# Storing the gated tile with a channel's four groups side by side, and reading its four shifted copies back in one transfer

## The chip, the cores and the metric

One core of one Trainium2 chip runs the whole kernel in one launch. The metric is device time in microseconds (us) of one execution, lower is better. Beside the plain timings there is one execution recorded by the hardware profiler; every row shown here is from that one. The engines are PE (matmul), DVE (vector), ACT (activation functions), POOL (a second elementwise engine) and SP, which here only issues transfers. A transfer issued by SP is spread over DMA engines, of which the core has 16.

## The reference, cut to what matters

Two layers of a diffusion transformer over 512 latent tokens and 256 context tokens, 1024 features, float32. The change touches the first layer's mixer alone, a convolution module that both streams pass through:

```
def conformer_conv(h, w_pw1, b_pw1, w_dw, b_dw, ln_g, ln_b, w_pw2, b_pw2):
    u = h @ w_pw1 + b_pw1
    a, g = jnp.split(u, 2, axis=-1)
    u = a * jax.nn.sigmoid(g)
    u = depthwise_conv(u, w_dw) + b_dw          # 31 taps per channel, over tokens
    u = jax.nn.silu(layer_norm(u, ln_g, ln_b))
    return u @ w_pw2 + b_pw2
```

After it come a gated feed-forward with a 3-tap convolution, then the second layer (neighbourhood attention and the same feed-forward).

## The kernel before

Everything is held with features on the 128 partitions and tokens along the row, so the 1024 features are 8 tiles. A matmul in float32 precision is made of three products of rounded parts (lines 1525 to 1527); for that ACT rounds every block of weights (`w_raw` to `w_hi`, line 757) and POOL makes the remainder (`w_lo`, line 611).

**The steps.** The first product and the convolution are run as 16 steps, `n` = 0 to 15: the 8 feature tiles of the context (256 tokens), then the 8 of the latents (512 tokens). In step `n` PE makes the two halves of the product (`pw1_step`, 2 x 24 matmuls), ACT takes the sigmoid of the second half, DVE multiplies it with the first into the gated tile `u` (`gated`, line 1247), and PE then does the convolution of the step before (`convolve(n - 1)`). In between PE does some unrelated matmuls for the modulation vectors, whose weights arrive as `ada_raw` (512 KB each, four buffers).

**The convolution.** A part of the 31 taps is done by PE, the rest by DVE directly on `u` (line 1223). On PE, four taps go in one matmul: the 128 rows of the moving operand are 32 channels in four copies, copy `i` shifted by `i` tokens, and the stationary operand `diag_w` holds the four taps on four 32-wide diagonals. A tile of 128 channels is four groups `j` of 32 channels, so a shifted buffer (`shifted_ctx`, `shifted_lat`, two of each) has partition `32 * i + b` and, in its row, the four groups `j` one behind the other. To bring channels `32 * j + b` onto partitions `32 * i + b`, SP stores `u` in DRAM (`u_dram`, two buffers a side) and reads it back four times.

**SP's order** is written by hand, `spread_u(n)`: wait for the gated tile (`glu`), wait that the last reading of this DRAM buffer has landed (`r_in`), store it, issue the two weight blocks of step `n + 3` (`step_loads`), wait until the store has landed (`u_out`), wait until the convolution two steps back has read its shifted buffer (`conv_pe`), issue the read-back, then issue up to two `ada_raw` loads. Ahead of the next `spread_u` there may be more `ada_raw` loads; together they are 3 a latent step and 1 a context step on average. All these transfers are on SP's one queue. `convolve(n)` waits for `r_in`.

Of the kernel before, what the change touches and what calls it, by code (L numbers as in the profile page):

```python
# [15 lines left out]
GROUPS, SHIFTS = 8, 4  # L16
PE_GROUPS = {"lat": 4, "ctx": 6}
DVE_TAP0 = SHIFTS * min(PE_GROUPS.values())
BLK32 = P // SHIFTS
# [5 lines left out]
LAT, CTX = "lat", "ctx"  # L25
# [46 lines left out]
def build(nc, shapes, rows_of, x_t, ctx_t, mod_w, mod_rows, cond_row, cv_w_pw1, cv_w_pw2, na_w_qkv, na_w_o, ffn_w_up, ffn_w_down,  # L72
          rpb_padded, vectors_in, taps_in, dve_taps_in, diag_in, ident_in, mask_in, out_t):
    L, C, D, F, HEADS, RPB_ROWS, RPB_COLS, TAPS = shapes
    N = {LAT: L, CTX: C}
    KD = D // P
    KF = F // P
# [83 lines left out]
    with stack:  # L161
        def sb(name, cols, dt=F32, on=stack):
            return on.enter_context(nc.sbuf_tensor(name, [P, cols], dt))

        def sem(name):
            return stack.enter_context(nc.semaphore(name))
# [45 lines left out]

        UW = {s: N[s] + 32 for s in N}
        RW = {s: N[s] + 28 for s in N}
        V, U, R, Yb, Ghi, Glo = {}, {}, {}, {}, {}, {}
        with ExitStack() as g:
            V[LAT], V[CTX] = sb("v_lat", KD * L, on=g), sb("v_ctx", KD * C, on=g)
            with ExitStack() as h:
                U[LAT] = [sb(f"u_lat{i}", UW[LAT], on=h) for i in range(2)]  # L220
                diag_w = [sb(f"diag_w{i}", GROUPS * SHIFTS * BLK32, on=h) for i in range(2)]
                taps_w = sb("taps_w", KD * GROUPS * SHIFTS, on=h)
                dve_taps = sb("dve_taps", KD * (GROUPS * SHIFTS - DVE_TAP0), on=h)
                diag = sb("diag", BLK32, on=h)
                glu_s = sb("glu_s", L, on=h)
                R[CTX] = [sb(f"shifted_ctx{i}", SHIFTS * RW[CTX], on=h) for i in range(2)]
                U[CTX] = [sb(f"u_ctx{i}", UW[CTX], on=h) for i in range(2)]
                R[LAT] = [sb(f"shifted_lat{i}", SHIFTS * RW[LAT], on=h) for i in range(2)]
                ada_raw = [sb(f"ada_raw{i}", 2 * 512, on=h) for i in range(ADA_RING)]
            with ExitStack() as h:  # L230
                Yb[LAT] = sb("yb_lat", KD * L, on=h)
                with ExitStack() as k:
                    Yb[CTX] = sb("yb_ctx", KD * C, on=k)
                Ghi[CTX] = sb("g_hi_ctx", KF * C, F32R, on=h)
                Glo[CTX] = sb("g_lo_ctx", KF * C, F32R, on=h)
            sb("first_room", KD * L + 2 * KF * C, on=g)
            ada_row = sb("ada_row", 512, on=g)
        with ExitStack() as g:
            Ghi[LAT] = sb("g_hi", KF * L, F32R, on=g)
# [1 line left out]
        with ExitStack() as g:  # L241
# [38 lines left out]
        u_dram = {s: [nc.dram_tensor(f"u_{s}_{i}", (P, UW[s]), F32, kind="Internal").ap() for i in range(2)]  # L280
                  for s in N}
# [4 lines left out]
        u_out = sem("u_out")  # L286
        r_in = {s: [sem(f"r_in_{s}{i}") for i in range(2)] for s in N}
# [130 lines left out]
        def side_of(n):  # L418

            return CTX if n < KD else LAT  # L420

        def pe_groups(n):

            return {STEPS - 1: GROUPS, STEPS - 2: GROUPS - 2}.get(n, PE_GROUPS[side_of(n)])
# [41 lines left out]
        def _(sp):  # L466
# [33 lines left out]
            def ada_loads(lists):  # L500
                for b in range(*lists):
                    if b + ADA_RING < CHUNKS * CHUNK_BLOCKS:
                        ada_load(b + ADA_RING)

            def spread_u(n):

                side, s, m = side_of(n), n % 2, n % KD
                uw, rw = UW[side], RW[side]
                sp.wait_ge(glu, n + 1)
                if m >= 2:  # L510
                    sp.wait_ge(r_in[side][s], 64 * (m // 2))
                sp.dma_start(u_dram[side][s][:, :], U[side][s][:, :]).then_inc(u_out, 16)
                step_loads(n + 3)
                sp.wait_ge(u_out, 16 * (n + 1))
                if n >= 2:
                    sp.wait_ge(conv_pe, n - 1)
                for i in range(SHIFTS):
                    d = u_dram[side][s]
                    src = bass.AP(tensor=d.tensor, offset=d.offset + i, ap=[[uw, BLK32], [BLK32 * uw, SHIFTS], [1, rw]])
                    dst = R[side][s][BLK32 * i:BLK32 * (i + 1), :].rearrange("p (j n) -> p j n", n=rw)  # L520
                    sp.dma_start(dst, src).then_inc(r_in[side][s], 16)
                ada_loads(ada_from[n][2])

            def step_loads(n):

                for half in range(2):
                    if n < STEPS:
                        ph = phases["pw1c" if n < KD else "pw1l"]
                        load(ph, n % KD // 2, 2 * (n % 2) + half, n % KD < 2)
                    else:  # L530
                        t = 2 * (n - STEPS) + half
                        load(phases["pw2c"], t // 4, t % 4, t < RING)
# [9 lines left out]
            for n in range(STEPS):  # L542
                for half in range(2):
                    ada_loads(ada_from[n][half])
                spread_u(n)
# [909 lines left out]
        def _(pe):  # L1455
# [27 lines left out]
            def convolve(n):  # L1483

                side, m, s = side_of(n), n % KD, n % 2
                w, rw = N[side], RW[side]
                pe.wait_ge(wd_rdy, n + 1)
                pe.wait_ge(r_in[side][s], 64 * (m // 2 + 1))
                if n >= 2:
                    pe.wait_ge(conv, n - 1)  # L1490
                groups = pe_groups(n)
                for g in range(groups):
                    for j in range(SHIFTS):
                        c = (g * SHIFTS + j) * BLK32
                        ins = pe.matmul(CONV[n % 2][BLK32 * j:BLK32 * (j + 1), 0:w], diag_w[s][:, c:c + BLK32],  # L1495
                                        R[side][s][:, j * rw + SHIFTS * g:j * rw + SHIFTS * g + w],
                                        start=(g == 0), stop=(g == groups - 1))
                ins.then_inc(conv_pe, 1)

            def pw1_step(n, extra=None):  # L1500

                ph, it, j = pw1_of(n)
                side = side_of(n)
                ready = normed("in_c" if side == CTX else "in_l") if n % KD == 0 else None
                for half in range(2):
                    split_wait(ph, it, j + half)
                    if half == 0 and n:
                        pe.wait_ge(glu, n)
                    products(bank[half][:, 0:N[side]], N[side], ph.slot(j + half), KD, Hhi[side], Hlo[side],
                             0, True, True, ready if half == 0 else None).then_inc(blk, 1)  # L1510
                    ada_products(ada_from[n][half])
                    if half == 0 and extra:
                        extra()
                if n:
                    convolve(n - 1)
                ada_products(ada_from[n][2])
# [180 lines left out]
            def last_convolution():  # L1697
                convolve(STEPS - 1)
                ada_turn(2)
# [158 lines left out]
            s = [ph.slot(j) for j in range(3)]  # L1858
# [107 lines left out]
```

## Time and profile before

| | us |
|---|---|
| median of 3 timed runs | 1746.15 |
| lowest and highest of them | 1746.05, 1753.84 |
| profiled execution | 1744.28 |
| its span, first to last instruction | 1742.5 |
| first store of a gated tile (step 0) | 62.83 |
| first store of a latent tile (step 8) | 159.32 |
| start of the last convolution (step 15) | 294.86 |
| PE busy, share of the span | 93% |

The 16 steps that the change touches thus lie in the first 305 us of the span. In the rows below a time is from the start of the span. The "DMA share" of a stretch is the busy share of the 16 DMA engines taken together (a packet's time can overlap the next one's, so it can come out slightly above 1), and GB/s is what they moved. PEclk is the granted TensorE clock as a part of 2.4 GHz.

### The profile page before, as it was taken

Reading aid. Unit: us, or ns where it says so; the run is one execution under the profiler, and the core shown is the slowest. Engines: PE = TensorE matmul, PEld = TensorE weight load, DVE = VectorE, ACT = ScalarE, POOL = GpSimd, SP = SyncE. Lnnn points to the kernel's source line nnn. Section 1 sums busy time; section 2 is a strip of 40 time slices with the busy share of each in tenths; the row PEclk is TensorE's granted clock in tenths of the full one; section 3 lists DMA queues with packets and bytes.
Section 4 is the critical chain, followed back from the end, with each engine's and each line's share of the span. In section 5 each row is a group of like instructions: output and inputs, shape, how many; then the busy total and the mean of one; then the engine's idle time right before and its main releaser. Section 6 shows DMA issues by size and latency. Waiting matters only on the chain.

```text
span 1742.5 us, 26261 instructions
## 1 busy us (share of the span) xinstructions
PE 1625.5 (93%) x9469; PEld 1310.2 (75%) x9469; DVE 712.8 (41%) x1396; ACT 748.8 (43%) x1126; POOL 791.0 (45%) x436
## 2 busy tenths in 40 slices
PE   4789998899899999999999799999987899999996
PEld 1666564779899988888888677788865788888884
DVE  0564796646662034444442524433342433333002
ACT  1532242546675445455322345444444444443220
POOL 0454334556679834444455334233326244444551
PEclk9899999999999999999999899999998899999998
DMA  7767787444456633233574111211203132333321
GB/s 250 274 202 218 213 236 218 157 146 130 145 172 180 184 97 96 97 90 91 226 278 161 50 37 50 79 42 43 67 25 109 49 97 96 96 96 89 96 81 49
DMA packets 70942, 222.63 MB, mean 128 GB/s; under 512 B 7888, under 2 KB 15568, under 8 KB 70608
## 3 DMA queue, kind: packets, MB, share of 16 engines
q1 hardware_dynamic: 69856, 219.91, 40.2%
q10 hardware_dynamic: 1008, 1.66, 0.3%
q8 instruction: 52, 0.85, 0.2%
q14 instruction: 26, 0.21, 0.0%
HBM read 216.03 MB, written 5.51 MB: 127 GB/s over the span
## 4 chain that ended last, share of the span: by engine, by line
PE 80%; issue 7%; DVE 5%; ACT 3%; DMA 2%; POOL 1%; DVEq 1%; ACTq 0%; SPq 0%; POOLq 0%
PE bank L1525 20%; PE bank L1527 20%; PE bank L1526 19%; PE bank L1735 3%; PE bank L1737 3%; PE bank L1736 3%; PE bank L1495 3%; PE bank L1813 2%; PE bank L1835 1%; PE bank L1823 1%; PE bank L1469 1%; DVE bank L1223 1%; PE bank L1665 1%; PE bank L1540 1%; DMA ada_raw<-in_mod_w 1%
## 5 line engine op out<-in xcount | busy, mean ns | idle before, releaser
L611 POOL TENSOR_TENSOR w_lo<-w_raw,w_hi 128x1024 fp32r<-128x1024 f32 (+1 forms) x284 | 668.3, 2359 | 810.0 <-ACT w_hi L757 809.8
L757 ACT ACTIVATE w_hi<-w_raw 128x1024 fp32r<-128x1024 f32 (+1 forms) x284 | 294.4, 1037 | 200.3 <-PE bank L1527 189.9
L1525 PE MATMUL bank<-h_hi_lat,w_hi 128*128 128x512 f32 x888 | 351.1, 395 | 5.1 <-DVE h_lo_lat L1182 4.5
L1527 PE MATMUL bank<-h_hi_lat,w_lo 128*128 128x512 f32 x888 | 349.4, 394 | 0.0
L1526 PE MATMUL bank<-h_lo_lat,w_hi 128*128 128x512 f32 x888 | 347.4, 391 | 0.0
L1525 PEld LDWEIGHTS bank<-h_hi_lat,w_hi 128*128 128x128 f32 x888 | 167.3, 188 | 53.6 <-issue 10.8
L1526 PEld LDWEIGHTS bank<-h_lo_lat,w_hi 128*128 128x128 f32 x888 | 167.2, 188 | 36.9
L1527 PEld LDWEIGHTS bank<-h_hi_lat,w_lo 128*128 128x128 f32 x888 | 167.2, 188 | 36.3
L1525 PE MATMUL bank<-h_hi_ctx,w_hi 128*128 128x256 f32 x560 | 166.8, 298 | 21.1 <-DVE g_lo_ctx L1367 10.2
L1526 PE MATMUL bank<-h_lo_ctx,w_hi 128*128 128x256 f32 x560 | 162.3, 290 | 0.0
L1527 PE MATMUL bank<-h_hi_ctx,w_lo 128*128 128x256 f32 x560 | 162.1, 289 | 0.0
L1527 PE MATMUL bank<-g_hi,w_lo 128*128 128x512 f32 x352 | 138.4, 393 | 0.0
L1525 PE MATMUL bank<-g_hi,w_hi 128*128 128x512 f32 x352 | 137.7, 391 | 0.0
L1526 PE MATMUL bank<-g_lo,w_hi 128*128 128x512 f32 x352 | 137.3, 390 | 0.0
L1525 PEld LDWEIGHTS bank<-h_hi_ctx,w_hi 128*128 128x128 f32 x560 | 111.4, 199 | 30.5 <-issue 13.0
L1354 DVE SCALAR_TENSOR_TENSOR bank<-gate_in,vectors,bank 128x512 f32<-128x512 f32 (+1 forms) x66 | 44.0, 666 | 170.4 <-ACT bank L911 170.0
L1526 PEld LDWEIGHTS bank<-h_lo_ctx,w_hi 128*128 128x128 f32 x560 | 111.0, 198 | 1.0 <-issue 1.0
L1527 PEld LDWEIGHTS bank<-h_hi_ctx,w_lo 128*128 128x128 f32 x560 | 111.1, 198 | 0.0
L1362 DVE TENSOR_TENSOR bank<-gate,bank 128x512 f32<-128x512 f32 (+1 forms) x66 | 40.1, 607 | 154.1 <-ACT gate L919 154.1
L1397 DVE CUSTOM_DVE_ANT_0 scores<-bank,bias 128x512 f32<-128x512 f32 x64 | 44.0, 687 | 103.3 <-issue 103.0
L1114 DVE RECIPROCAL root<-root 128x128 f32<-128x128 f32 x6 | 5.7, 953 | 190.3 <-ACT root L781 190.3
L637 POOL TENSOR_TENSOR feature_sum_lat<-feature_sum_lat,sq 128x512 f32<-128x512 f32 x32 | 41.8, 1306 | 88.2 <-ACT sq L883 88.1
(192 smaller groups left out, 2690.8 us busy)
## 6 DMA issues: line engine op xcount, KB each, us to landing
w_raw<-in_ffn_w_up SPq DMA_DIRECT2D x132, 512.0 KB, 3.6
ada_raw<-in_mod_w SPq DMA_DIRECT2D x64, 512.0 KB, 5.6
w_raw<-in_cv_w_pw SPq DMA_DIRECT2D x48, 512.0 KB, 5.1
w_raw<-in_ffn_w_down SPq DMA_DIRECT2D x48, 448.0 KB, 3.5
mod_rows<-in_mod_rows SPq DMA_DIRECT2D x32, 512.0 KB, 5.6
w_raw<-in_ffn_w_down SPq DMA_DIRECT2D x24, 512.0 KB, 3.7
w_raw<-in_na_w_qkv SPq DMA_DIRECT2D x24, 512.0 KB, 5.7
shifted_lat<-u_lat SPq DMA_DIRECT2D x32, 270.0 KB, 6.8
```

The lines of the kernel that those rows point to most:

```text
L611: pool.tensor_tensor(wlo[s][:, 0:kt * P], raw[s][:, 0:kt * P], whi[s][:, 0:kt * P].bitcast(F32), ALU.subtract).then_inc(w_lo, 1)
L637: pool.tensor_tensor(acc[side][:, :], acc[side][:, :], src, ALU.add).then_inc(done, 1)
L757: act.activation(whi[s][:, 0:kt * P], raw[s][:, 0:kt * P], ACT.Copy).then_inc(w_hi, 1)
L1354: dve.scalar_tensor_tensor(tp, g_in[:, 0:n], vcol("ffn_w_dw", m + layer * 3 * KF), tp, ALU.mult, ALU.add).then_inc(tap, 1)
L1397: dve.tensor_tensor_reduce(out=scores[par][:, :], in0=SCORES[hp][:, :], in1=bias[hp][:, n * 512:(n + 1) * 512], scale=1.0, scalar=-3e38, o ...
L1495: ins = pe.matmul(CONV[n % 2][BLK32 * j:BLK32 * (j + 1), 0:w], diag_w[s][:, c:c + BLK32], R[side][s][:, j * rw + SHIFTS * g:j * rw + SHIFT ...
L1525: pe.matmul(b, whi[s][:, w], hi[:, a], start=(first and k == 0), stop=False)
L1526: pe.matmul(b, whi[s][:, w], lo[:, a], start=False, stop=False)
L1527: ins = pe.matmul(b, wlo[s][:, w], hi[:, a], start=False, stop=(last and k == kts - 1))
L1735: pe.matmul(b, whi[s][:, w], hi[:, a], start=(k == 0), stop=False)
L1736: pe.matmul(b, whi[s][:, w], lo[:, a], start=False, stop=False)
L1737: ins = pe.matmul(b, wlo[s][:, w], hi[:, a], start=False, stop=(k == KD - 1))
```

## The change

The DRAM copy is laid out channel by channel, a channel `b`'s four groups `j` side by side (each `uw` long: 288 numbers for the context, 544 for the latents), where it was laid out like the tile. The store has the same 128 rows in SBUF; on the DRAM side it is now a pattern of 4 by 32 rows. The read-back is one transfer in place of four: 128 rows of `4 * uw - 4` numbers (4592 bytes for the context, 8688 for the latents) in place of 4 x 128 rows of `uw - 4` numbers (1136 and 2160 bytes). Its DRAM side is a pattern of 4 shifts by 32 channels, its SBUF side the 128 partitions. The semaphore `r_in` then rises by 16 a tile and not by 64, the step from group to group in a shifted buffer is `uw` and not `uw - 4`, and the shifted buffers are 12 numbers wider.

```diff
-        RW = {s: N[s] + 28 for s in N}
+        RW = {s: SHIFTS * UW[s] - SHIFTS for s in N}
...
-                uw, rw = UW[side], RW[side]
+                uw, d = UW[side], u_dram[side][s]
                 sp.wait_ge(glu, n + 1)
                 if m >= 2:
-                    sp.wait_ge(r_in[side][s], 64 * (m // 2))
-                sp.dma_start(u_dram[side][s][:, :], U[side][s][:, :]).then_inc(u_out, 16)
+                    sp.wait_ge(r_in[side][s], 16 * (m // 2))
+                rows = bass.AP(tensor=d.tensor, offset=d.offset, ap=[[uw, SHIFTS], [SHIFTS * uw, BLK32], [1, uw]])
+                sp.dma_start(rows, U[side][s][:, :]).then_inc(u_out, 16)
                 step_loads(n + 3)
                 sp.wait_ge(u_out, 16 * (n + 1))
                 if n >= 2:
                     sp.wait_ge(conv_pe, n - 1)
-                for i in range(SHIFTS):
-                    d = u_dram[side][s]
-                    src = bass.AP(tensor=d.tensor, offset=d.offset + i, ap=[[uw, BLK32], [BLK32 * uw, SHIFTS], [1, rw]])
-                    dst = R[side][s][BLK32 * i:BLK32 * (i + 1), :].rearrange("p (j n) -> p j n", n=rw)
-                    sp.dma_start(dst, src).then_inc(r_in[side][s], 16)
+                src = bass.AP(tensor=d.tensor, offset=d.offset,
+                              ap=[[1, SHIFTS], [SHIFTS * uw, BLK32], [1, SHIFTS * uw - SHIFTS]])
+                sp.dma_start(R[side][s][:, :], src).then_inc(r_in[side][s], 16)
...
-                w, rw = N[side], RW[side]
+                w, rw = N[side], UW[side]
...
-                pe.wait_ge(r_in[side][s], 64 * (m // 2 + 1))
+                pe.wait_ge(r_in[side][s], 16 * (m // 2 + 1))
```

SP's queue, steps 3 and 4 (context). A row gives the line, the tile written and read, and the shape on the written side. Before:

```order
L512 DMA u_ctx<-u_ctx 128x288 [waits r_in_ctx1,glu]
L479 DMA w_raw<-in_cv_w_pw 128x1024 [waits w_lo] x2
L521 DMA shifted_ctx<-u_ctx 32x4x284 [waits conv_pe,u_out]
L521 DMA shifted_ctx<-u_ctx 32x4x284 x3
L498 DMA ada_raw<-in_mod_w 128x1024 [waits ada_blk] x2
L512 DMA u_ctx<-u_ctx 128x288 [waits r_in_ctx0,glu]
```

With the change:

```order
L513 DMA u_ctx<-u_ctx 4x32x288 [waits r_in_ctx1,glu]
L479 DMA w_raw<-in_cv_w_pw 128x1024 [waits w_lo] x2
L520 DMA shifted_ctx<-u_ctx 128x1x1148 [waits conv_pe,u_out]
L498 DMA ada_raw<-in_mod_w 128x1024 [waits ada_blk] x2
L513 DMA u_ctx<-u_ctx 4x32x288 [waits r_in_ctx0,glu]
```

Three issues a step are gone, and nothing else has changed its place. The store writes 4 x 32 rows where it wrote 128; the read-back writes all 128 partitions at once.

SP's queue, steps 9 and 10 (latents). Before:

```order
L512 DMA u_lat<-u_lat 128x544 [waits glu]
L479 DMA w_raw<-in_cv_w_pw 128x1024 [waits w_lo] x2
L521 DMA shifted_lat<-u_lat 32x4x540 [waits conv_pe,u_out]
L521 DMA shifted_lat<-u_lat 32x4x540 x3
L498 DMA ada_raw<-in_mod_w 128x1024 [waits ada_blk] x2
L512 DMA u_lat<-u_lat 128x544 [waits r_in_lat0,glu]
```

With the change:

```order
L513 DMA u_lat<-u_lat 4x32x544 [waits glu]
L479 DMA w_raw<-in_cv_w_pw 128x1024 [waits w_lo] x2
L520 DMA shifted_lat<-u_lat 128x1x2172 [waits conv_pe,u_out]
L498 DMA ada_raw<-in_mod_w 128x1024 [waits ada_blk] x2
L513 DMA u_lat<-u_lat 4x32x544 [waits r_in_lat0,glu]
```

The same holds here. The `bias_table` loads of the attention, which the change doesn't touch, are the only transfers of the program before with a pattern like that of the new read-back: 8 by 16 rows in DRAM, 128 partitions of one row of 265 numbers in SBUF.

```
src = bass.AP(tensor=rpb_padded.tensor, offset=it * (4 * RPB_HEAD) + (2 * j + hp) * RPB_HEAD,
              ap=[[RPB_COLS, P // NA_KW], [1, NA_KW], [1, RUN]])
sp.dma_start(table[:, hp * RUN:(hp + 1) * RUN], src).then_inc(tab_in, 16)
```

## Rows read from the trace of the kernel before

**Rows 1.** The page: the span, busy time by engine, and 40 slices.

```profile
span 1742.5 us, 26261 instructions
...
PE 1625.5 (93%) x9469; PEld 1310.2 (75%) x9469; DVE 712.8 (41%) x1396; ACT 748.8 (43%) x1126; POOL 791.0 (45%) x436
...
PE   4789998899899999999999799999987899999996
...
DMA  7767787444456633233574111211203132333321
```

**Rows 2.** Longest waits of PE from 60 to 305 us: total us, times, longest.

```profile
PE bank L1495 <- issue: 15.5, 4, 4.5
PE bank L1525 <- POOL w_lo L611: 2.9, 1, 2.9
```

**Rows 3.** Chain of waits in that stretch, the waits at convolutions: start, us, what.

```profile
92.27 3.03 issue
...
113.17 3.73 issue
...
136.66 4.22 issue
...
290.32 4.54 issue
```

**Rows 4.** Timeline of SP's queue: start, us, line, tiles, count. First and last steps.

```profile
62.83 0.33 SPq L512 DMA_DIRECT2D u_ctx<-u_ctx  x1
...
85.45 0.33 SPq L512 DMA_DIRECT2D u_ctx<-u_ctx  x1
...
90.17 1.75 SPq L521 DMA_DIRECT2D shifted_ctx<-u_ctx  x4
...
159.32 0.33 SPq L512 DMA_DIRECT2D u_lat<-u_lat  x1
...
230.44 0.33 SPq L512 DMA_DIRECT2D u_lat<-u_lat  x1
```

**Rows 5.** Timeline of PE: two convolutions of latent steps.

```profile
212.46 3.64 PE L1495 MATMUL bank<-shifted_lat,diag_w 128*32 128x512 f32 x32
...
228.84 3.64 PE L1495 MATMUL bank<-shifted_lat,diag_w 128*32 128x512 f32 x32
```

**Rows 6.** Transfers by kind: count, KB each, median us from issue to landing.

```profile
w_raw<-in_cv_w_pw SPq DMA_DIRECT2D x48, 512.0 KB, 5.1
...
shifted_lat<-u_lat SPq DMA_DIRECT2D x32, 270.0 KB, 6.8
shifted_ctx<-u_ctx SPq DMA_DIRECT2D x32, 142.0 KB, 4.5
...
u_lat<-u_lat SPq DMA_DIRECT2D x8, 272.0 KB, 2.3
...
bias_table<-in_rpb_padded SPq DMA_DIRECT2D x16, 132.5 KB
```

**Rows 7.** Stretches: bounds, length, busy by engine, PEclk, DMA share, GB/s.

```profile
166.00:168.00 2.00, 2.00 (x13) 0.72 (x11) 0.01 (x1) 0.80 (x1) 0.00 (x0) 1.00 1.07 213
...
1203.00:1205.00 2.00, 2.00 (x13) 1.41 (x10) 1.78 (x8) 0.61 (x2) 0.00 (x0) 1.00 0.96 389
...
1161.00:1162.30 1.30, 1.30 (x8) 1.04 (x7) 1.18 (x6) 1.09 (x3) 0.74 (x1) 1.00 0.47 94
1234.90:1235.90 1.00, 1.00 (x6) 0.82 (x5) 0.90 (x5) 0.81 (x3) 0.70 (x1) 1.00 0.45 92
```

**Rows 8.** Timeline of SP's queue around the third of these stretches.

```profile
1159.58 1.46 SPq L491 DMA_DIRECT2D bias_table<-in_rpb_padded  x2
1161.60 1.50 SPq L479 DMA_DIRECT2D w_raw<-in_na_w_qkv  x3
```

**Rows 9.** Two stretches of the context steps, columns as in rows 7.

```profile
130.00:141.00 11.00, 6.78 (x68) 6.11 (x64) 6.83 (x11) 5.13 (x8) 5.73 (x4) 1.00 0.86 261
141.00:152.00 11.00, 11.00 (x80) 6.98 (x77) 7.09 (x10) 0.81 (x2) 3.64 (x2) 0.84 0.52 146
```

More of the change, by code:

```diff
@@ L225, in build @@
                 glu_s = sb("glu_s", L, on=h)
-                R[CTX] = [sb(f"shifted_ctx{i}", SHIFTS * RW[CTX], on=h) for i in range(2)]
+                R[CTX] = [sb(f"shifted_ctx{i}", RW[CTX], on=h) for i in range(2)]
                 U[CTX] = [sb(f"u_ctx{i}", UW[CTX], on=h) for i in range(2)]
-                R[LAT] = [sb(f"shifted_lat{i}", SHIFTS * RW[LAT], on=h) for i in range(2)]
+                R[LAT] = [sb(f"shifted_lat{i}", RW[LAT], on=h) for i in range(2)]
                 ada_raw = [sb(f"ada_raw{i}", 2 * 512, on=h) for i in range(ADA_RING)]
@@ L235, in build @@
                 Glo[CTX] = sb("g_lo_ctx", KF * C, F32R, on=h)
-            sb("first_room", KD * L + 2 * KF * C, on=g)
+            sb("first_room", KD * L + 2 * KF * C + 32, on=g)
             ada_row = sb("ada_row", 512, on=g)
```

## The prediction

> **What bounds the kernel now.** I read the page first: PE is busy for 93% of a span of 1742.5 us, and the slices show where it is not: among the few below 9 tenths are the first seven, and there the DMA engines are at 7 tenths and more [rows 1]. The change lies in exactly this part. Then the list of PE's waits between 60 and 305 us: 15.5 us in 4 waits stand at line 1495, the convolution, more than at all other lines together [rows 2]. The chain of waits gives their places, three in context steps and one before the last convolution, and calls them "issue", that is, no single releaser [rows 3]. Two rows of SP's queue say what the second half of it is: in step 2 the store goes out at 85.45 and the read-back only at 90.17, since SP waits for the store to land, and the convolution begins at 92.27 + 3.03 = 95.30, when the last of four readings has landed [rows 3, 4]. So the store and the read-back are already the late ones in four of 16 steps.
>
> One lap, from the first store (62.83) to the last convolution (290.32 + 4.54 = 294.86), takes 232.0 us: 96.5 us for the 8 context steps, 12.1 each, and 135.5 us for the 8 latent steps, 16.9 each [rows 3, 4]. This is the stretch that the change can lengthen or shorten.
>
> **What the change saves.** Three issues a step on SP: four take 1.75 us, so about 1.3 us of SP's time, of which 0.4 may be lost again, because the two issues of the similar bias_table pattern take 1.46 us, 0.73 each [rows 4, 8]. The read-back also leaves the form in which it fills only 32 partitions at a time. While those run, 213 GB/s are moved at a share of 1.07, 213 / (1.07 x 16) = 12.4 GB/s for each busy engine; weight blocks that fill all 128 partitions go at 389 / (0.96 x 16) = 25.3 GB/s [rows 7]. The copies' bytes are the same but for 12 numbers a row. PE, DVE, ACT and POOL have the same instructions of the same shapes, so I cost the wider step between groups and the moved buffers at nothing: a convolution reads the same 512 numbers a row and keeps its 3.64 us [rows 5].
>
> **What the change costs.** Both new transfers have a DRAM side whose outermost count is 4: the store 4 x 32 rows, the read-back 4 x 32. No transfer of before has that. The nearest is bias_table: outermost count 8 on the DRAM side, 128 partitions in SBUF. Two stretches show it in flight alone. It is issued at 1159.58, the weights behind it at 1161.60, and from 1161.0 to 1162.3 the DMA engines are busy 0.47 of the time (had the weights begun to arrive, the share would only be too high); at 1234.9 it is 0.45 [rows 7, 8]. Weights, with 128 as outermost count on both sides, show 0.96. I read this as: 8 of the 16 engines work on it, one for each outermost step, and the new transfers will be worked on by 4.
>
> The Trainium skill says so outright ("DMA: Bandwidth & Descriptors", section "Why a DMA increments its semaphore by 16 and not by 1"): a DMA runs on the largest number of engines, up to 16, that divides the slowest dimension of both sides, and on this path on the lowest-numbered ones. By that rule both transfers use the same 4 engines; the trace's 0.47 and 0.45 agree with its 8 for bias_table. The same page's list "Rules for kernel authors" also advises one large transfer for many small ones; by that alone the sum would be the second rival's below.
>
> Now the load on one of these 4 engines in one step, by bytes. Every 512 KB block (2 of weights, and ada_raw 3 times a latent and once a context step) [rows 6] is spread over all 16, 32.8 KB each, 1.30 us at 25.3 GB/s: 6.5 us a latent step, 3.9 us a context step. The store is 32 rows of 2176 bytes on each of the 4, 69.6 KB (context 32 x 1152 = 36.9 KB). The read-back is 32 rows of 8688 bytes, 278 KB (context 32 x 4592 = 147 KB). Before, they were 17 and 69 KB.
>
> The pace of a busy engine is the disputed price. At best it is the 25.3 GB/s of the weights: a latent step is then 6.5 + 2.8 + 11.0 = 20.3 us, a context step 3.9 + 1.5 + 5.8 = 11.2 us. At worst it is the 12.4 of the readings that crowd into 32 partitions, or the 94 / (0.47 x 16) = 12.5 and 92 / (0.45 x 16) = 12.8 of bias_table [rows 7]: latent 6.5 + 5.6 + 22.2 = 34.3, context 3.9 + 3.0 + 11.8 = 18.7. Each of the 4 engines would walk down a block of 32 partitions, side by side. bias_table is the nearest row in form, but its rows have 1060 bytes, and the trace has no long rows in that form, so I take 15 GB/s, near the slow end: latent 6.5 + 4.6 + 18.5 = 29.6, context 3.9 + 2.5 + 9.8 = 16.2.
>
> Is this load on the path? All is on one queue, so each engine works it off in order. SP issues the store of step n + 1 when PE has done the products after convolution n - 1: 228.84 - 212.46 = 16.4 us from convolution to convolution, and 230.44 - 228.84 = 1.6 us more to the store, 18.0 us [rows 4, 5]. Convolution n - 1 starts when read-back n - 1 has landed. From that landing the 4 engines have a whole step's work before them, 29.6 us, and the next store comes after 18.0: they never run empty, and a latent step takes what their load takes. The latency between store and read-back (a store now lands 2.3 us after its issue, of which most is not transfer [rows 6]) is covered by the two weight blocks behind the store, 2.6 us. In a context step it is 12.1 against 16.2, the same. The next weights still come in time, since they lie ahead of the read-back and are wanted two steps later.
>
> The sum: 8 x 16.2 + 8 x 29.6 = 366 us in place of 232, with nothing to give it back later, because PE is the bound from 305 us on and its work is the same. That is +134 us. The profiled execution, 1744.28 us (span 1742.5), would become 1878; the median of the runs is 1.9 above it, 1746.15 + 134 = **1880 us**.
>
> PE will idle in these steps. Its granted clock may then be below 1 for a part: in before, a stretch with 6.78 of 11 us busy is followed by one at 0.84 [rows 9]. At 0.84 the 18.0 us become about 21, still below 29.6, so I add nothing. If the pace is the fast one, this cover is gone, and it could cost up to 1 us a latent step.
>
> **The rivals.**
> 1. *Four engines, at the full pace.* The blocks do not get in each other's way, since engines drift apart. For it speaks that the rows are long. Context steps then stay at their 12.1, latent ones take 20.3: 96.5 + 162 = 259, +27, **1773 us**; with the clock's price 1781.
> 2. *All 16 engines share it, faster than before.* The mechanism would be that the SBUF side's 128 partitions decide, and bias_table's 0.47 comes from its short rows. Then the read-back goes at 16 x 25.3 = 405 GB/s over all partitions, 1.45 us instead of 2.8 in a context step and 2.75 instead of 5.2 in a latent step, and 1.2 us earlier by the issues saved. It takes 2.5 us from three waits and 3.7 from the fourth, which are 3.03 to 4.54 long [rows 3]: -11 us, **1735 us**. The point from which it decides is the engine count: with 8 engines at full pace the latent read-back takes 5.5 us, as long as now; only above that is there a gain. Against it: those two shares, since short rows would make a busy engine slow, not idle.
> 3. *The middle.* With 8 engines the latent load is 6.5 + 11.6 = 18.1 us, about PE's lap, and the context load 10: a little over PE's 16.9, near **1750 us**.
>
> **How the numbers follow.** Four engines near the slow pace 0.60, at the full pace 0.26, all 16 engines 0.10, something near no change 0.04. The likeliest gives 1880. Its bounds are 12.5 GB/s (8 x (18.7 + 34.3) = 424, +192, 1938) and the first rival (1773); both cases hold 0.86, so the range is 1773 to 1940. A change below 0.5%, 9 us, is about what a measurement of this kernel can't tell from none. Faster by more than that is rival 2, 0.10; within it rival 3, 0.04; slower 0.86.
>
> **What would show it.** In the profile after: DMA share in the read-back's stretches at 0.25 to 0.35 and some 60 GB/s, where now it is above 1 at 213; latent stores about 30 us apart; landing of shifted_lat 15 us and more; PE's waits at the convolution in nearly all 16 steps, 130 us in sum; from the second product on, nothing changed. A share near 1 and a landing under 5 us would prove the step on the engine count wrong; stores 20 us apart the step on the pace.

## The result: 8.2% slower

| | median us | ratio to before, 95% interval |
|---|---|---|
| before, the same chips | 1746.85 | |
| with the change | 1889.96 (1884.2 to 1898.4, 6 runs) | 1.0821 [1.0791, 1.0852] |

The forecast was 1880 us in a range of 1773 to 1940. The profiled execution of the change has a span of 1889.7 us, 147.2 more than before.

The page of the changed kernel: the span, the busy time by engine, and 40 slices of the span in tenths of busy time. They answer to [rows 1].

```profile
span 1889.7 us, 26213 instructions
...
PE 1650.1 (87%) x9469; PEld 1315.5 (70%) x9469; DVE 715.3 (38%) x1396; ACT 748.6 (40%) x1126; POOL 789.3 (42%) x436
...
PE   4757656567998999999999979999999699999996
...
PEclk9888877788999999999999989999999799999998
DMA  7554565554434465332328721121121222333321
```

The instruction counts of the engines are those of before. What has changed is the first quarter: PE is at 5 to 7 tenths in slices 2 to 9 (about 47 to 425 us), and the DMA engines, far from being fuller, are down to about 5 tenths. Both sides idle. This fits a transfer that a few engines carry while the others have nothing to do; the stretches below show it.

Longest waits of PE from 60 to 460 us (in total, times, longest), which answer to [rows 2]:

```profile
PE bank L1494 <- issue: 135.2, 12, 16.6
PE bank L1494 <- DMA shifted_ctx<-u_ctx: 4.7, 1, 4.7
PE bank L1524 <- POOL w_lo L610: 4.2, 1, 4.2
```

15.5 us in 4 waits have become 139.9 us in 13, all at the convolution (line 1495 is 1494 now). The difference, 124 of the 147 us, is the change's cost seen from PE. Most of the rest goes with PE's clock: PE was busy 24.6 us more (1650.1 against 1625.5) with the same 9469 matmuls, and the granted clock is lower in the slices in which it waits.

The chain of waits in the same stretch (start, us, what), two of the waits and the convolutions behind them; compare [rows 3]:

```profile
274.02 9.74 issue
283.75 5.27 PE bank L1494 x32
...
421.99 15.74 issue
437.73 8.51 PE bank L1494 x64
```

And SP's queue (start, us, line, tiles), which answers to [rows 4]:

```profile
61.18 0.68 SPq L513 DMA_DIRECT2D u_ctx<-u_ctx  x1
...
189.38 0.55 SPq L513 DMA_DIRECT2D u_lat<-u_lat  x1
...
256.21 0.54 SPq L520 DMA_DIRECT2D shifted_lat<-u_lat  x1
...
337.19 0.55 SPq L513 DMA_DIRECT2D u_lat<-u_lat  x1
...
366.96 0.55 SPq L513 DMA_DIRECT2D u_lat<-u_lat  x1
...
415.77 0.54 SPq L520 DMA_DIRECT2D shifted_lat<-u_lat  x1
```

The lap from the first store to the last convolution is 437.73 - 61.18 = 376.5 us, where it was 232.0: +144.5, nearly all of the 147.2. The context steps take (189.38 - 61.18) / 8 = 16.0 us each (12.1 before), the latent ones (437.73 - 189.38) / 8 = 31.0 (16.9 before). The first two latent stores are 16.0 us apart, and from the second on each comes 27.8 to 35.7 us after the one before; the pair shown is 29.8. The last read-back, issued at 415.77, lets PE go at 437.73, 22.0 us later. The one issued at 256.21, with more queued ahead of it, takes until 283.75.

Stretches of the changed kernel in which little else is in flight (bounds, length, busy by engine, PEclk, DMA share, GB/s), to be held against [rows 7]:

```profile
174.00:176.00 2.00, 2.00 (x27) 1.15 (x20) 0.50 (x1) 0.00 (x0) 0.00 (x0) 0.89 0.25 79
...
274.00:276.00 2.00, 0.02 (x1) 0.00 (x0) 0.75 (x1) 1.95 (x3) 0.24 (x1) 1.00 0.25 61
424.00:426.00 2.00, 0.00 (x0) 0.00 (x0) 0.00 (x0) 1.99 (x6) 0.74 (x2) 1.00 0.23 74
```

A share of 0.25 is 4 engines of 16. At 61 GB/s each of the four moves 15 GB/s, at 74 it is 74 / (0.23 x 16) = 20, at 79 in a context step 20.

Three more stretches show what the read-back's own do not:

```profile
223.00:227.00 4.00, 4.00 (x26) 1.25 (x19) 0.29 (x1) 0.00 (x0) 0.00 (x0) 0.67 0.26 102
415.40:417.00 1.60, 1.60 (x16) 0.93 (x9) 0.76 (x2) 0.00 (x0) 0.00 (x0) 1.00 0.11 46
186.60:190.50 3.90, 3.90 (x58) 2.38 (x60) 0.75 (x1) 2.00 (x3) 0.90 (x1) 1.00 0.00 0
```

In the first, a read-back has landed (PE went on at 220.45) and the next is issued only at 227.99; the four engines carry the store and what is left of the loads, at 102 / (0.26 x 16) = 25 GB/s each. In the second, a store has landed and the read-back that waited for it is just being issued: fewer than two engines are busy on average. In the third, at the end of the context steps, nothing is in flight at all.

### The profile page after: what moved, and what is told of

It is laid out like the page before. It is cut to its first block, busy times and chain, and to the rows that moved or that the text cites. A ratio compares the mean times of both kernels' runs of the same rounds, so it can differ in the third digit from the quotient of the medians.

```text
span 1889.7 us, 26213 instructions
## 1 busy us (share of the span) xinstructions
PE 1650.1 (87%) x9469; PEld 1315.5 (70%) x9469; DVE 715.3 (38%) x1396; ACT 748.6 (40%) x1126; POOL 789.3 (42%) x436
## 4 chain that ended last, share of the span: by engine, by line
PE 77%; issue 12%; DVE 3%; ACT 3%; DMA 3%; POOL 1%; DVEq 1%; ACTq 0%; POOLq 0%
PE bank L1524 19%; PE bank L1526 18%; PE bank L1525 18%; PE bank L1494 4%; PE bank L1734 3%; PE bank L1736 3%; PE bank L1735 3%; PE bank L1812 2%; PE bank L1468 2%; PE bank L1834 1%; PE bank L1822 1%; PE bank L1664 1%; PE bank L1539 1%; DMA ada_raw<-in_mod_w 1%; ACT w_hi L756 1%
## 5 line engine op out<-in xcount | busy, mean ns | idle before, releaser
L1524 PE MATMUL bank<-h_hi_lat,w_hi 128*128 128x512 f32 x888 | 351.7, 396 | 4.5 <-DVE h_lo_lat L1181 4.5
L1494 PE MATMUL bank<-shifted_lat,diag_w 128*32 128x512 f32 x304 | 52.6, 858 | 102.5 <-issue 102.5
L1524 PEld LDWEIGHTS bank<-h_hi_ctx,w_hi 128*128 128x128 f32 x560 | 110.8, 198 | 32.2 <-issue 15.5
L1494 PEld LDWEIGHTS bank<-shifted_lat,diag_w 128*32 128x32 f32 x304 | 13.5, 150 | 137.4 <-issue 137.4
```

Source lines behind the costliest of these rows:

```text
L1524: pe.matmul(b, whi[s][:, w], hi[:, a], start=(first and k == 0), stop=False)
```

## The experiments

All but e5 and e6 compute what the reference does; those two read back rows that the convolution does not want, and are there for their times alone. Ratios are to the kernel before, run beside them (its median was 1749.59 us beside e1 to e4 and 1748.66 beside e5 to e8). A lap is the time from the first store to the start of the last convolution in the profiled execution. The rest of the span is 1507 to 1518 us in all ten profiles, so the laps hold the large differences, but one of some us in a single profile says little: e4's lap is 3.6 us shorter than before's, its span 4.1 us longer, and its profiled execution was the slowest of its seven.

| kernel | store, engines | read-back, engines | median us | ratio | lap us |
|---|---|---|---|---|---|
| before | 1 issue, 16 | 4 issues, 16 | 1746.85 | | 232.0 |
| the change | 1, 4 | 1, 4 | 1889.96 | 1.0821 | 376.5 |
| e1_store_only | 1, 4 | 4, 16 | 1763.43 | 1.0088 [1.0062, 1.0114] | 246.4 |
| e2_read_only | 4, 16 | 1, 4 | 1864.07 | 1.0658 [1.0606, 1.0711] | 351.7 |
| e3_both16 | 4, 16 | 4, 16 | 1751.27 | 1.0009 [0.9983, 1.0035] | 239.1 |
| e4_order32 | 4, 16 | 1, 16 | 1740.11 | 0.9938 [0.9917, 0.9960] | 228.4 |
| e5_two_engines | 4, 16 | 1, 2 | 1925.37 | 1.0997 [1.0965, 1.1029] | 409.4 |
| e6_eight_engines | 4, 16 | 1, 8 | 1782.39 | 1.0189 [1.0158, 1.0221] | 264.9 |
| e7_order32_store4 | 1, 4 | 1, 16 | 1748.91 | 0.9992 [0.9975, 1.0010] | 236.5 |
| e8_short128 | 1, 16 | 4, 16 | 1741.18 | 0.9954 [0.9935, 0.9974] | 226.8 |

The engine counts are the theory's (the largest number up to 16 that divides the outermost counts of both sides); the stretches show 2, 4, 8 and 16.

The trace also records each packet, the piece that one engine moves at a time, and here a row of a store or of a read-back is one packet. Its time gives the pace of one busy engine without any dividing by a share. These are medians over the 16 steps:

| kernel | latent read-back row | GB/s | context read-back row | GB/s |
|---|---|---|---|---|
| before: 32 partitions at a time, 16 engines | 2160 bytes, 174 ns | 12.4 | 1136 bytes, 81 ns | 14.0 |
| e3: the same, long rows | 8688 bytes, 649 ns | 13.4 | 4592 bytes, 325 ns | 14.1 |
| the change: 128 partitions, 4 engines | 8688 bytes, 652 ns | 13.3 | 4592 bytes, 184 ns | 25.0 |
| e6: 128 partitions, 8 engines | 8688 bytes, 698 ns | 12.4 | 4592 bytes, 255 ns | 18.0 |
| e5: 128 partitions, 2 engines | 8688 bytes, 331 ns | 26.2 | 4592 bytes, 178 ns | 25.8 |
| e4: 128 partitions, 16 engines | 8688 bytes, 328 ns | 26.5 | 4592 bytes, 178 ns | 25.8 |
| e8: 128 partitions, 16 engines | 2160 bytes, 88 ns | 24.5 | 1136 bytes, 51 ns | 22.3 |

The latent store's row of 2176 bytes takes 91 ns in before, 89 ns on the change's 4 engines, and 143 to 153 ns where it goes in four issues of 32 partitions (e2, e3, e4).

**e1_store_only**, against the change: the read-back in four issues, still of long rows (the waits for `r_in` count to 64 again; here and below such changes of counts are left out of the cuts shown).

```diff
-                src = bass.AP(tensor=d.tensor, offset=d.offset,
-                              ap=[[1, SHIFTS], [SHIFTS * uw, BLK32], [1, SHIFTS * uw - SHIFTS]])
-                sp.dma_start(R[side][s][:, :], src).then_inc(r_in[side][s], 16)
+                for i in range(SHIFTS):
+                    src = bass.AP(tensor=d.tensor, offset=d.offset + i, ap=[[SHIFTS * uw, BLK32], [1, SHIFTS * uw - SHIFTS]])
+                    sp.dma_start(R[side][s][BLK32 * i:BLK32 * (i + 1), :], src).then_inc(r_in[side][s], 16)
```

> The store as in the change (4 by 32 rows on the DRAM side), the read-back in four transfers again, each of 32 long rows whose outermost count is 32. If the number of engines is the outermost count, only the store runs on 4 engines: 69.6 KB on each, 3 us where it took 1, so the 4 engines carry about 15 us a latent step against PE's 16.9 and are not the bound; the store only lands 1 to 3 us later, which counts in the steps where the convolution waited already. Expected 1750 to 1770 us. If the store were the costly half, it would be most of the 144 us: above 1850.

Measured 1763.43 us, inside. The store alone, with the layout, costs 0.88%; against e3, which has the layout too, it is 0.8%. How it costs is seen on SP's queue:

```profile
161.98 0.52 SPq L513 DMA_DIRECT2D u_lat<-u_lat  x1
162.54 1.12 SPq L479 DMA_DIRECT2D w_raw<-in_cv_w_pw  x2
169.58 1.72 SPq L520 DMA_DIRECT2D shifted_lat<-u_lat  x4
```

The read-back goes out 7.6 us after the store, where in step 12 of before it was 2.4 us (230.44 to 232.82). The list of SP's waits has it for all eight latent steps, 47.9 us of waiting for the store to land; in before the same row is 7.3 us:

```profile
SPq L520 <- DMA u_lat<-u_lat: 47.9, 8, 6.3
```

```profile
SPq L521 <- DMA u_lat<-u_lat: 7.3, 8, 1.0
```

I had expected the store to land 1 to 3 us later; it is (47.9 - 7.3) / 8 = 5.1. What was missing is that the two weight blocks issued right behind it use the same four engines before it is through. Its rows run from 163.14 to 169.21 us by the packet records, with packets of the weight blocks between them, and towards the end little more than four engines are busy, at the full pace:

```profile
167.00:169.00 2.00, 2.00 (x10) 1.63 (x10) 1.56 (x4) 0.00 (x0) 0.00 (x0) 1.00 0.29 99
```

The store's 69.6 KB and the weights' 2 x 32.8 KB on one engine are 5.3 us at 25.3 GB/s (an estimate), where the store alone would be 2.8.

**e2_read_only**, against the change: the store in four issues of 32 partitions.

```diff
-                rows = bass.AP(tensor=d.tensor, offset=d.offset, ap=[[uw, SHIFTS], [SHIFTS * uw, BLK32], [1, uw]])
-                sp.dma_start(rows, U[side][s][:, :]).then_inc(u_out, 16)
+                for j in range(SHIFTS):
+                    rows = bass.AP(tensor=d.tensor, offset=d.offset + j * uw, ap=[[SHIFTS * uw, BLK32], [1, uw]])
+                    sp.dma_start(rows, U[side][s][BLK32 * j:BLK32 * (j + 1), :]).then_inc(u_out, 16)
...
-                sp.wait_ge(u_out, 16 * (n + 1))
+                sp.wait_ge(u_out, 64 * (n + 1))
```

> The read-back as in the change (one transfer, 4 by 32 rows on the DRAM side), the store in four transfers of 32 partitions, which gives each an outermost count of 32. By the theory the 4 engines lose the store's 2.2 us a latent step and 1.2 a context step of the 31.0 and 16.0 measured: about 345 us from first store to last convolution, 1855 to 1870 us. By the rival, that the order of the rows in DRAM or their length is what costs and not the engine count, it would be the same as the change, 1890, or fall only with e3.

Measured 1864.07 us, inside. The read-back is the costly half, 6.6%; with e1's 0.9% they make 7.5 of the 8.2%.

**e3_both16** has both edits: the change's layout and its long rows, all with outermost count 32.

> The change's layout in DRAM and its long rows, but store and read-back each in four transfers of 32 partitions, outermost count 32. If engine count is all, this is the time of before within 0.5%: 1740 to 1756 us, perhaps a few us more for SP's three further issues. If long overlapping rows or the new layout cost by themselves, it stays well above: 1780 or more.

Measured 1.0009 [0.9983, 1.0035]. The layout, the long rows and three more store issues a step together cost nothing that can be measured. All of the loss is gone with the outermost count of 4.

**e4_order32** keeps the single read-back, but turns the order of its rows, so that 32 channels are outermost and the four shifts of a channel lie on neighbouring partitions. The tap constants and the diagonal are laid out to match.

```diff
-                              ap=[[1, SHIFTS], [SHIFTS * uw, BLK32], [1, SHIFTS * uw - SHIFTS]])
+                              ap=[[SHIFTS * uw, BLK32], [1, SHIFTS], [1, SHIFTS * uw - SHIFTS]])
...
-    dw = dw.reshape(GROUPS, SHIFTS, D // P, SHIFTS, BLK32).transpose(1, 4, 2, 0, 3)
+    dw = dw.reshape(GROUPS, SHIFTS, D // P, SHIFTS, 32, BLK32 // 32).transpose(4, 1, 5, 2, 0, 3)
...
-    diag_in = give("diag", np.tile(np.eye(BLK32, dtype=np.float32), (SHIFTS, 1)))
+    diag_in = give("diag", np.eye(BLK32, dtype=np.float32).reshape(32, 1, BLK32 // 32, BLK32).repeat(SHIFTS, axis=1).reshape(P, BLK32))
```

> As e2, but the copies lie channel by channel (partition 4b + i, with tap and diagonal constants in that order), so the one transfer of 128 long rows has 32 as its outermost count on the DRAM side. If the outermost count sets the engines, it runs on 16: at 12 to 25 GB/s an engine 2.75 to 5.6 us for a latent tile in place of 20. Expected 1730 to 1750 us, faster than before if engines don't share ports. If it is the single transfer of long rows that is slow, it stays at 1855 to 1870 as e2.

Measured 0.9938 [0.9917, 0.9960], 1740.11 us: faster than before, and 124 us faster than e2, which brings in the same 128 rows in another order, and so onto other partitions. The step on the engine count stands. While this read-back runs in a latent step, with the loads queued around it:

```profile
164.00:168.00 4.00, 4.00 (x22) 2.41 (x21) 0.00 (x0) 1.06 (x1) 2.26 (x1) 1.00 0.96 392
```

And e3, which has the same bytes in 32-partition pieces:

```profile
170.00:174.00 4.00, 4.00 (x22) 2.35 (x21) 0.00 (x0) 1.06 (x1) 2.33 (x1) 1.00 1.00 206
```

All 16 engines are busy in both, yet e3 moves half as much, like the read-back of before at 213 GB/s [rows 7]. (e4's stretch holds weight loads as well; by the row times it is 328 against 649 ns.)

**e5_two_engines** and **e6_eight_engines** test the disputed pace. Against e2, the DRAM side of the read-back:

```diff
-                              ap=[[1, SHIFTS], [SHIFTS * uw, BLK32], [1, SHIFTS * uw - SHIFTS]])
+                              ap=[[1, 2], [124 * uw // 63, P // 2], [1, SHIFTS * uw - SHIFTS]])
```

```diff
-                              ap=[[1, SHIFTS], [SHIFTS * uw, BLK32], [1, SHIFTS * uw - SHIFTS]])
+                              ap=[[1, 8], [8 * uw, P // 8], [1, SHIFTS * uw - SHIFTS]])
```

> As e2, but the read-back's DRAM side is 2 by 64 rows of the same length, so that its outermost count is 2 (the rows that it reads are then not the right ones; all else is computed as before). Two theories of the pace. If the 4 engines of e2 get in each other's way, two by two, because blocks of partitions 32 apart share something, then two engines on partitions 0 to 63 and 64 to 127 go at the full 25 GB/s: 556 KB each in 22 us, a latent step about 30 us, a context step 16, and the time is that of e2, 1864, within 20. If a row of 8688 bytes just takes 640 ns when few engines carry it, a latent step is 41 + 8 us, a context step 20, and the time above 2000.

> As e5, with 8 by 16 rows: outermost count 8 (again the wrong rows). Half the load of e2 on each engine. At the slow pace a latent step's load is 6.5 + 1.1 + 10.4 = 18 us, just over PE's 16.9, a context step's below 12: 1755 to 1775 us. At the full pace, or with 16 engines for some other reason, 1745 to 1755.

Measured 1925.37 and 1782.39 us, and both miss: the first lies between the two theories, 40 us above the one and 75 below the other, the second 7 us above its range. The stretches settle what the times leave open. Two engines, the read-back alone in flight:

```profile
452.00:455.00 3.00, 0.00 (x0) 0.00 (x0) 0.00 (x0) 2.97 (x6) 1.51 (x2) 0.82 0.12 52
467.00:470.00 3.00, 0.00 (x0) 0.00 (x0) 0.00 (x0) 0.00 (x0) 0.00 (x0) 0.50 0.12 50
```

Eight engines:

```profile
323.00:325.00 2.00, 0.00 (x0) 0.00 (x0) 0.00 (x0) 1.48 (x3) 2.00 (x1) 0.50 0.46 109
```

The share is 2/16 and 8/16. Two engines move 52 / (0.12 x 16) = 27 GB/s each, the full pace; eight move 109 / (0.46 x 16) = 14.8 each, four 15 to 20 (above), sixteen in e4 392 / (0.96 x 16) = 25.5. So a long row isn't slow in itself, nor are few engines. The slow ones are the counts 4 and 8, where, if each engine has a block of partitions, the blocks are 32 or 16 long. With two they would be 64 long, and the pace is full. For e5 my steps of 16 and 30 us add up to a lap of 368 us, and it was 409.4; its profile says where the 41 us are. SP's queue in it:

```profile
63.01 1.27 SPq L514 DMA_DIRECT2D u_ctx<-u_ctx  x3
```

```profile
204.88 1.73 SPq L514 DMA_DIRECT2D u_lat<-u_lat  x4
206.65 0.93 SPq L479 DMA_DIRECT2D w_raw<-in_cv_w_pw  x2
```

The chain at its last convolution:

```profile
451.95 20.42 issue
```

A context step takes (204.88 - 63.01) / 8 = 17.7 us where I had 16, a latent one (451.95 + 20.42 - 204.88) / 8 = 33.4 where I had 30. What fills the 1.7 and 3.4 I did not separate; the stores and loads that share the two engines with the read-back are in it, and so is any gap between the store's landing and the read-back.

e6's miss is in the latent steps:

```profile
163.65 1.73 SPq L514 DMA_DIRECT2D u_lat<-u_lat  x4
```

```profile
318.70 9.20 issue
```

They take (318.70 + 9.20 - 163.65) / 8 = 20.5 us where I had 18, and the context steps 12.6. A mean row of 730 ns, where I had 650 (10.4 us for 16 rows), makes 1.3 of the 2.5 us; the rest is open.

One thing the two don't separate. In e2, e5 and e6, if each engine has one step of the outermost count, the engines work at the same time on rows that start one number apart in DRAM; in e4 and e8, if each engine takes neighbouring rows, they read different channels. So the slow pace could also arise where the DRAM side is read, and not where the partitions are written. Two facts speak for the partitions: e5 reads overlapping rows too and is at full pace, and before and e3 are slow with rows of different channels. No run gives 4 engines rows that are far apart.

**e7_order32_store4** is e4 with the change's store.

> e4's read-back (outermost count 32) with the change's own store (4 by 32 rows, one issue). Against e4 it says what the 4-engine store costs where the read-back is fast: the store lands 1 to 3 us later and takes 1.3 us less to issue. e1 against e3 was 12 us; here 5 to 12, so 1745 to 1752 us, no better than before.

Measured 0.9992 [0.9975, 1.0010]. Against e4 the 4-engine store costs 0.5%, about what the fast read-back had won.

**e8_short128** leaves layout and store of before alone. Each of the four read-backs brings one group in its four shifts to all 128 partitions, with constants as in e4.

```diff
-                for i in range(SHIFTS):
-                    d = u_dram[side][s]
-                    src = bass.AP(tensor=d.tensor, offset=d.offset + i, ap=[[uw, BLK32], [BLK32 * uw, SHIFTS], [1, rw]])
-                    dst = R[side][s][BLK32 * i:BLK32 * (i + 1), :].rearrange("p (j n) -> p j n", n=rw)
-                    sp.dma_start(dst, src).then_inc(r_in[side][s], 16)
+                d = u_dram[side][s]
+                for j in range(SHIFTS):
+                    src = bass.AP(tensor=d.tensor, offset=d.offset + j * BLK32 * uw, ap=[[uw, BLK32], [1, SHIFTS], [1, rw]])
+                    sp.dma_start(R[side][s][:, j * rw:(j + 1) * rw], src).then_inc(r_in[side][s], 16)
```

> Before's layout in DRAM and before's store of 128 rows in one issue; the read-back in four transfers, but each brings one group of 32 channels in its four shifts to all 128 partitions (channel by channel, outermost count 32) where before each brought one shift to 32 partitions. 16 engines and no crowding on either side, short rows. If the crowding is what the row pace showed, a latent read-back takes half as long, and the store 1 us where e4's takes 2. Expected 1732 to 1742 us, at least as fast as e4; if long rows and the single issue were what made e4 faster, it is the time of before.

Measured 0.9954 [0.9935, 0.9974], 1741.18 us, as fast as e4 (the intervals overlap). The bytes, the row length, the four issues and the 16 engines are those of before. What differs is which rows go in one issue, and with it where they land: one group in four shifts on 128 partitions, and not four groups in one shift on 32. While its read-back runs, with some weight loads beside it:

```profile
160.50:164.00 3.50, 3.50 (x19) 1.96 (x18) 0.89 (x2) 1.06 (x1) 0.24 (x1) 1.00 1.01 350
```

350 GB/s against 213, and 88 ns a row against 174. So neither the long rows nor the single issue is needed for e4's gain; filling all 128 partitions at once is enough.

## Why the prediction was right, point by point

- **What bounds the kernel**: right, though I misread the slices: of the first seven only four are below 9 tenths, and DMA's third is at 6 [rows 1]. The convolution's waits were already the longest, and the kernels that lost much lost it there: 15.5 us of such waits in before, 35.2 and 5.0 in e6, 135.2 and 4.7 in the change.
- **Engine count from the outermost count**: right, shown by the shares 0.12, 0.25 and 0.46, by e3 and above all by e4 against e2. That was the step on which everything hung, and its only evidence had been bias_table's 0.47 and 0.45 [rows 7]. The Trainium skill's rule ("DMA: Bandwidth & Descriptors", section "Why a DMA increments its semaphore by 16 and not by 1") holds in all four counts tried, and its advice in "Rules for kernel authors" to make one large transfer of many small ones did not pay here, where each of the four was 270 KB already: one transfer in place of four lost 6.6% with an outermost count of 4, and with 32 it was no faster than four (e4 0.9938, e8 0.9954).
- **The load of a latent step**: forecast 29.6 us, measured 31.0, and part of the closeness is luck, since three terms are off both ways. The read-back's rows take 638 ns on average, 32 of them 20.4 us where the sum had 18.5. The store was costed at the slow pace, 4.6 us, but its rows take 89 ns, 2.8 us in all. And the latency between the store's landing and the read-back was taken as covered, but in such a gap of 1.6 us only 0.11 x 16 = 1.8 of the four engines are busy on average (415.40).
- **The engines never run empty**: true for most of a latent step, apart from that gap. It is false for the context steps: at 186.60 to 190.50 and in shorter stretches before that the share is 0.00. There the forecast of 16.2 us, measured 16.0, was right for a reason that doesn't hold: a step is not only the engines' load, which is smaller than forecast (the read-back's 32 rows average 246 ns, 7.9 us for 9.8), but holds stretches in which PE is still making the next gated tile. What else is in the 16.0 us I did not separate. The loads on all 16 engines were costed at 25.3 GB/s, which doesn't hold beside the read-back either: from 432 to 434 us, with weight blocks queued behind the last read-back (issued from 416.35 on), the share was 0.90 at only 185 GB/s:

```profile
432.00:434.00 2.00, 0.00 (x0) 0.00 (x0) 0.00 (x0) 0.00 (x0) 0.00 (x0) 0.50 0.90 185
```

- **The clock**: PE's granted clock did fall, to 0.50 (1.2 GHz) late in each long wait, and a convolution of a latent step took 5.3 to 6.4 us instead of 3.64. I added nothing for it, and that was not quite right: where the DMA engines had run empty, PE was what the step waited for, and PE's 24.6 us more of busy time are part of the 147. How much of them the sum should have had I can't say.
- **Rivals**: the full pace (1773 us) is excluded by the 61 GB/s; all 16 engines (1735 us) by the share of 0.25. e4 does what the second rival described, and its 1740 us are near that rival's price. But the price was to come from four waits, 3.7 us of it from the last, and that one is 4.05 us in e4 where it was 4.54; e4's waits at the convolution are 11.9 us in sum against 15.7. So the agreement is not shown to have the forecast reason.

## What to carry to other kernels

Look at the outermost count of both sides of a transfer before its size: one of 4 leaves 12 of 16 DMA engines out, and whatever else is spread over all 16 has its share behind it on the four. Where the rows can be enumerated in another order, put a dimension outermost whose count is a multiple of 16; here 32 in place of 4 turned +6.6% into -0.6%. And let one transfer touch all 128 partitions rather than a block of 32: it halved the time of a row, from 174 to 88 ns, and e8, which does only that, is the version to keep. It is 0.5% faster than before and can't be told from e4.

## What the runs showed that I had not expected

- The small store is not small: 278 KB on 4 engines held the read-back back by 5 us a latent step and cost 0.5 to 0.8% (e7 against e4, e1 against e3), half a percent being all that a good read-back wins.
- Two engines were only 3.3% slower than four (1925 against 1864 us). Four had half the bytes each, but only half the pace, 13.4 against 26.2 GB/s.
- The wait before the last convolution, 4.54 us in before [rows 3], is still 3.19 us in e8 and 4.05 in e4, with read-back rows that take half the time. Why it is not shorter stays open. The chain of e8 and of e4 there:

```profile
285.77 3.19 issue
```

```profile
287.61 4.05 issue
```
